# A two-block transformer kernel on one core: the output projection of the merged mixers split into two halves of its input rows

## What is computed

```
# one layer of the second block (hx, hc: normed and modulated latent and context tokens)
r_lat, r_ctx = bidirectional_scan(retention inputs)        # 4 heads of 128
g_lat, g_ctx = bidirectional_scan(gated linear attention inputs)   # 4 heads: keys 64, values 128
ret = from_heads(head_layernorm(r)) * silu(parts[3])       # 512 columns
gla = from_heads(rmsnorm(g, gla_norm_g)) * silu(parts[7])  # 512 columns
mx  = concatenate([ret, gla], axis=-1)                     # 1024 columns
x   = x + g1 * (mx @ w_out)                                # w_out: 1024 x 1024
x   = x + g2 * squared_relu_mlp(modulate(rmsnorm(x)), w_mlp1, w_mlp2)
```

## Time and profile before

| | us |
|---|---|
| runs | 3664.37, 3665.28, 3668.57 |
| profiled execution | 3674.53 |
| its span | 3672.7 |
| PE busy | 3476.8 (95%) |
| DVE busy | 2018.7 (55%) |
| ACT busy | 1198.1 (33%) |
| POOL busy | 213.0 (6%) |

### The profile page before, as it was taken

The page is one execution under the profiler, slowest core; times in us unless marked ns, Lnnn a source line. Parts: engine busy times, 40 slices in busy tenths (PEclk is TensorE's granted clock), DMA queues, the critical chain, the costliest instruction groups (busy, mean ns, idle before and its releaser), DMA issues.

```text
span 3672.7 us, 42155 instructions
## 1 busy us (share of the span) xinstructions
PE 3476.8 (95%) x17456; PEld 2763.4 (75%) x17456; DVE 2018.7 (55%) x3717; ACT 1198.1 (33%) x2005; POOL 213.0 (6%) x302
## 2 busy tenths in 40 slices
PE   7989999999989999998999879999998998889998
PEld 6647688887867688887986557888886885568886
DVE  5564588786654587784136754333235236654334
ACT  5353432225453432223112233322233112144332
POOL 0200000001130000000000001000001000000000
PEclk9999999999999999999999869999999998789999
DMA  5302244443202244443210011121222220113331
GB/s 168 105 19 86 69 151 159 152 135 98 65 29 89 69 150 159 151 136 131 83 56 31 22 53 56 58 69 58 62 65 87 100 70 18 41 51 99 93 102 59
DMA packets 214107, 317.00 MB, mean 86 GB/s; under 512 B 5304, under 2 KB 162618, under 8 KB 212636
## 3 DMA queue, kind: packets, MB, share of 16 engines
q1 hardware_dynamic: 198108, 243.00, 20.7%
q0 software_dynamic: 15808, 71.31, 5.8%
HBM read 300.66 MB, written 14.49 MB: 86 GB/s over the span
## 4 chain that ended last, share of the span: by engine, by line
PE 87%; DVE 7%; ACT 3%; issue 2%; DMA 1%; POOL 0%; SPq 0%; DVEq 0%; ACTq 0%; POOLq 0%
PE ps L94 86%; DVE t L115 3%; ACT t L100 3%; DVE t L107 2%; PE ps L97 1%; DVE t L111 1%; DVE t L121 0%; DVE t L112 0%; DVE ps L115 0%; DMA t<-gates_away 0%; DVE t L125 0%; DVE t L118 0%; DVE ps L107 0%; DMA t<-in_mem 0%; ACT L100 0%
## 5 line engine op out<-in xcount | busy, mean ns | idle before, releaser
L94 PE MATMUL ps<-t,t 128*128 128x512 f32 (+5 forms) x17040 | 3421.3, 366 | 165.2 <-DVE t L115 56.7
L94 PEld LDWEIGHTS ps<-t,t 128*128 128x128 f32 (+3 forms) x17040 | 2712.4, 190 | 848.0 <-issue 169.2
L100 ACT ACTIVATE t<-t 128x512 f32<-128x512 f32 (+4 forms) x1146 | 812.3, 744 | 1290.6 <-PE ps L94 932.5
L107 DVE TENSOR_TENSOR t<-t,t 128x1024 fp32r<-128x1024 f32 (+6 forms) x826 | 742.4, 927 | 591.9 <-ACT t L100 576.2
L100 ACT ACTIVATE t<-ps 128x512 f32<-128x512 f32 (+7 forms) x442 | 221.9, 529 | 809.6 <-PE ps L94 767.9
L115 DVE SCALAR_TENSOR_TENSOR t<-t,t,t 128x256 f32<-128x256 f32 (+3 forms) x927 | 437.6, 534 | 13.7 <-ACT t L100 7.3
L107 DVE TENSOR_TENSOR t<-ps,t 128x512 f32<-128x512 f32 (+4 forms) x293 | 188.6, 660 | 207.7 <-PE ps L94 142.6
L115 DVE SCALAR_TENSOR_TENSOR t<-ps,t,t 128x512 f32<-128x512 f32 (+1 forms) x228 | 139.8, 662 | 278.7 <-PE ps L94 258.5
L118 DVE COPY t<-ps 128x256 f32<-128x256 f32 (+3 forms) x162 | 73.1, 479 | 272.6 <-PE ps L94 252.9
L107 POOL TENSOR_TENSOR t<-t,t 128x64 f32<-128x64 f32 (+1 forms) x196 | 130.1, 689 | 1580.9 <-ACT t L100 1577.8
L100 ACT ACTIVATE t<-t,t 128x512 fp32r<-128x512 f32 (+3 forms) x160 | 96.1, 603 | 194.2 <-DVE t L107 127.8
(11 more groups left out here) (33 smaller groups left out, 294.7 us busy)
## 6 DMA issues: line engine op xcount, KB each, us to landing
t<-in_w_ff SPq DMA_DIRECT2D x64, 1024.0 KB, 5.4
t<-in_w_mlp SPq DMA_DIRECT2D x64, 1024.0 KB, 5.5
t<-in_ada_w POOLq DMA_DIRECT2D x48, 1024.0 KB, 5.9
t<-in_w_in SPq DMA_DIRECT2D x30, 1024.0 KB, 5.4
t<-in_w_qkv_o SPq DMA_DIRECT2D x12, 1024.0 KB, 5.2
t<-in_w_mem_kv SPq DMA_DIRECT2D x8, 1024.0 KB, 6.4
t<-in_w_mem_q SPq DMA_DIRECT2D x8, 1024.0 KB, 5.1
t<-in_w_mem_o SPq DMA_DIRECT2D x8, 1024.0 KB, 5.1
```

What stands on the lines that cost most here:

```text
L94: return Issued(self, self.e and self.e.matmul(o, l, r, start=start, stop=stop, skip_group_check=True))
L100: return Issued(self, self.e and self.e.activation(o, i, f, **kw))
L107: return Issued(self, self.e and self.e.tensor_tensor(o, a, b, op))
```

## The change

The projection is cut by its input rows. `U.out2r[l]` takes rows 0 to 511 (retention), `U.out2[l]` rows 512 to 1023 (GLA); each has two blocks of 4 input tiles by 512 columns, so two pairs a block. A pair of such a half has 4 kk x 2 tiles x 3 terms = 24 matmuls of 512 columns (and 24 of 256 in layer 0). The four pairs of retention's half are new units in the mixer's list: `product` (PE runs the pair, DVE and ACT do `start`) and `add` (DVE adds to the residual). GLA's half stays where the projection was. All of `add_to` is done twice, once for each half.

Retention's units gain a step `half` (the split into hi and lo, in place: the buffer `H.RH` lies over `H.Q` and `H.K`), and are spread over fewer units of GLA: all but the last 15 in layer 0 and the last 10 in layer 1. The squares of the sums use `SQ` in place of `H.KS`, so that `c_back` no longer waits for the last `gnormed`.

```diff
-    def feat(i, ms, segs, c0s=None):
+    def feat(i, ms, segs, c0s=None, bases=None):
...
-            base = 3 * setno[0]
+            base = 3 * setno[0] if bases is None else bases[x // 2]
...
-        U.out2[l] = [feat(i, two(b), segs) for b, i in enumerate(cols(A["w_out_2"][l], q4))]
+
+        U.out2r[l], U.out2[l] = ([feat(block(A["w_out_2"][l], k0, 4, 512 * b, 512), list(range(4 * b, 4 * b + 4)), segs,
+                                       None, bases) for b in range(2)]
+                                 for k0, bases in ((0, (0, 0) if l == 0 else (0, 2)), (4, None)))
...
-    H.KS = [place([128, S], F, YB + 2048 * i) for i in range(2)]
+
+    H.RH = place([128, 2, 4, T], R, D1)
...
-        n = len(g) - 8
+        n = len(g) - (15 if l == 0 else 10)
+        behind = ({("work", 1, 9): "o0", ("sum", 2): "a0", ("work", 1, 11): "o1", ("sum", 4): "a1 o2", ("sum", 6): "a2 o3",
+                   ("sum", 8): "a3"} if l == 0 else
+                  {("work", 1, 5): "o0", ("work", 1, 6): "o1", ("work", 1, 7): "a0 o2", ("sum", 1): "a1 o3", ("sum", 3): "a2",
+                   ("sum", 4): "a3"})
...
+        def out_half(u):
+
+            if u[0] == "product":
+                use = U.out2r[l][u[1] // 2]
+                feature(use, H.RH, lambda kk: [("clo", l, kk, z) for z in range(len(segs))], [use.pairs[u[1] % 2]])
+
...
+            elif u[0] == "half":
+                h, z = u[1:]
+                t0, n = segs[z]
+                act.wait_ge("fdone", l, h, z)
+                act.activation(H.RH[:, 0, h, t0:t0 + n], H.K[:, h, t0:t0 + n], ACT.Copy).then_inc("chi", l, h, z)
...
-            if u == ("work", 1, len(work) - 1):
-
-                act.wait_ge("gout", l, 1, *work[-1])
-                for k in range(4):
-                    for z, (t0, n) in enumerate(segs):
-                        act.wait_ge("fdone", l, k, z)
-                        act.activation(HR2[:, 0, k, t0:t0 + n], H.Q[:, k, t0:t0 + n], ACT.Copy).then_inc("chi", l, k, z)
...
+            elif u[0] == "half":
+                h, z = u[1:]
+                t0, n = segs[z]
+                dve.wait_ge("chi", l, h, z)
+                dve.tensor_tensor(H.RH[:, 1, h, t0:t0 + n], H.K[:, h, t0:t0 + n], H.RH[:, 0, h, t0:t0 + n].bitcast(F),
+                                  ALU.subtract).then_inc("clo", l, h, z)
+
...
+        def out_half(u):
+            use = U.out2r[l][u[1] // 2]
+            if u[0] == "product":
+                start(use)
+            else:
+                add_to(use, streams, lambda m, z: (("x_back", "c_back")[z], l), gain1, use.pairs[u[1] % 2])
...
             if l == 0:
                 pl.wait_ge("decay_log", l, 3, 3)
-                pl.wait_ge("gnormed", l, len(gla_sums(l)) - 1)
                 pl.wait_ge("fdone", l, 3, len(segs) - 1)
                 pl.dma_start(CX, A["c_away"].rearrange("p (k t) -> p k t", k=8)).then_inc(s_cback, "c_back", l)
```

More of the change, by code:

```diff
@@ L357, in program @@
         U.ff[l] = mlp(A["w_ff1"][l], A["w_ff2"][l], lat)
[L358 removed]
+    U.rq, U.rk, U.rv, U.rg, U.gq, U.gk, U.kt, U.gv, U.gg, U.gd, U.out2r, U.out2, U.ff2 = ({} for _ in range(13))
     for l in range(2):
@@ L493, in ret_units @@
         tasks, out_ = ret_tasks(l), []
-        steps = ([("mean", 0, 1), ("mean", 1, 2), ("var", 0, 3), ("end", 0, 5), ("var", 1, 5), ("end", 1, 6)] if l == 0 else
-                 [("mean", 0, 1), ("var", 0, 3), ("end", 0, 5)])
+        steps = ([("mean", 0, 1), ("mean", 1, 2), ("var", 0, 3), ("end", 0, 5), ("var", 1, 5), ("end", 1, 6), ("half", 0, 6),
+                  ("half", 1, 7)] if l == 0 else [("mean", 0, 1), ("var", 0, 3), ("end", 0, 5), ("half", 0, 5)])
         for h in range(4):
@@ L556, in mixed_units @@
             y = min(len(r), len(r) * (x + 1) // n)
+            out_ += [("out", ("product" if v[0] == "o" else "add", int(v[1]))) for v in behind.get(u, "").split()]
+        return out_
         return out_
@@ L575, in weights, with feature @@
             return [hl[:, a, :].rearrange("p (k n) -> p k n", k=u.kc) for a in range(2)]
-        def feature(u, x, ready_k):
+        def feature(u, x, ready_k, pairs=None):
             wv = weights(u)
-            for pair in u.pairs:
+            for pair in u.pairs if pairs is None else pairs:
                 for kk in range(u.kc):
@@ L1361, in project_out @@
                 start(u)
-                for m in two(b):
+                for m in [t.m for t in u.tiles]:
                     for s, (dst, n) in enumerate(streams):
@@ L1768, in hybrid_scalar @@
         for mixer, u in mixed_units(l):
-            (ret if mixer == "ret" else gla)(u)
+            {"ret": ret, "gla": gla, "out": out_half}[mixer](u)
         gla_high(len(sums) - 1)
         for z in range(2):
-            sq_free[z], rs_free[z] = ("rpv", l, len(tasks) - 1), ("fdone", l, 3, len(segs) - 1)
+            sq_free[z], rs_free[z] = ("gnormed", l, len(sums) - 1), ("fdone", l, 3, len(segs) - 1)
         streams = [(X, S), (CX, C)][:len(segs)]
@@ L1920, in attention, with add_to @@
                 prep(h, 4)
-        def add_to(u, streams, after=None, gain=None):
-            for t in u.tiles:
+        def add_to(u, streams, after=None, gain=None, tiles=None):
+            for t in u.tiles if tiles is None else tiles:
                 dve.wait_ge(*ready(u, t))
```

41 lines of the change are left out of this document (20 added, 21 removed).

## The result

The changed kernel takes 3695.45 us, the median of four runs (3687.69 to 3698.39). The kernel before took 3666.93 us beside it (3664.37 to 3673.72). The ratio is 1.0072, 95% interval 1.0051 to 1.0093: 0.7% slower, by some 26 us. The forecast was 3669 us with a range up to 3684. The measured time lies 11 us beyond that range. What was called within the noise (+3.8 us) is a clear loss of 26 to 29 us.

A forecast was written before the change was run, and what follows sets the result against it. The prediction took PE's matmuls, 87% of the chain, as the bound, so a change pays only where PE waits or runs slowly. Layer 0 +6.6 and layer 1 -2.8 gave +3.8 us on 3665.3: 3669 us, range 3648 to 3684.

The forecast's parts named there:

- The tail of layer 0: From work 8's end to the projection's end: 103.2 us plus 5 for the clock against 111.3, so -3.1 us.
- The four waits: Layer 0's tail: PE idle 3.0, 5.4, 4.6 and 5.8 us, 18.8 in all, each ended by DVE's adds.
- The clock term: Layer 0's tail: time lost at clock 0.50 after the four waits, 5 us within 0 to 9.3.
- The front of layer 0: Layer 0's mixer up to work 8: DVE takes on 11.4 us, partly in holes; +5 us within 0 to 11.4.
- theory O: From the experiments, not the forecast: layer 0's front lengthens by which unit an end stands in front of; order alone, 10 to 15 us.
- POOL's order in layer 0: The residual is issued before the last gates, so DVE waits for the gates: +4.7 us within 0 to 9.0.
- Layer 1: Tail +0.2, halves +3.5, gate wait gone -6.5: -2.8 us in all.
- The gain of 6.5 us that I booked for the wait: Layer 1's mixer: residual issued earlier, so PE's share of the wait for the gates goes; bounds 3 and 9 us.
- the 3.5 us that I had put against it: Layer 1's mixer: cost of the halves, where DVE waits for ACT's copy and subtracts; bounds 0 and 5.8 us.
- The base: Whole kernel: profiled execution 3674.5 us, median of the runs 9.2 us lower, so +3.8 us was added to 3665.3.
- Rival 2: Mixers of both layers: VectorE bounds, all 17.2 us of added work lands on the path, 3678 us; chance 0.20.
- Rival 3: Tails of both layers: the clock takes its full price, 9.3 + 6 us in place of 8, 3676 us; chance 0.10.

The follow-up runs named there:

- b1: The kernel before, unedited, run again for a profile nearer its median: 3666.93 us, -2.0 us (0.9997) against the kernel before beside it.
- a1: The changed kernel, unedited, run again: 3695.29 us, +25.7 us (1.0071) over the kernel before.
- b2: The kernel before with eight (layer 0) and four (layer 1) empty half units in retention's list, so only the order shifts: +7.2 us (1.0021) over the kernel before.
- a2: The kernel before with only retention's units spread over 15 (layer 0) and 10 (layer 1) fewer linear-attention units, not 8; no split: +12.4 us (1.0040) over the kernel before.
- d1: b2 with layer 0's retention ends and the steps behind them held past cumulations, states and work 0, in both directions: -0.7 us (0.9996) against the kernel before.
- d2: The changed kernel with all retention units held past work 0 from the first such end on, in layer 0's first direction: +19.7 us (1.0044) over the kernel before.
- d3: d2 with the same rule in layer 0's second direction too, the residual issued later: +21.5 us (1.0048) over the kernel before.
- c4: The changed kernel with POOL issuing the gates in front of the residual in both layers: +23.9 us (1.0061) over the kernel before.

## Why the prediction was wrong, step by step

**The tail of layer 0: right within 3.3 us, in part by luck.** Forecast -3.1 us. Measured -3.4 us between the two first traces (119.3 to 115.9) and +0.2 between b1 and a1. The four waits came where I had written them, each ended by DVE's adds: 1.9, 4.6, 3.9 and 5.1 us with the second short wait of each, 15.6 us for the forecast 18.8. The clock term was too small. I had taken it between what follows a wait of 2.04 us (3.4 us at 0.50) and one of 6.26 us (6.0 us), but each of these shorter waits was followed by 6.8 us at 0.50, with PE busy for 5.8 to 6.0 us of them. That is 2.9 to 3.0 us lost each time, 11.7 in all, not 5 within 0 to 9.3. In the first trace this came out even because the clock was at 1.00 from 2160.0 to the first of these waits: product 0 had no slow beginning, and PE was at that wait 18.1 us after work 8, not 21.5. In a1 the clock was low for longer there, and it took 20.9 us. Terms were off in opposite directions.

**The front of layer 0: wrong, and it decides the case.** Forecast +5 for DVE's added work, within 0 to 11.4, and +4.7 for the gates. Measured +23.6 (first traces) and +28.8 (b1 and a1). The step that failed is the one that took 5 us, within 0 to 11.4, for the 11.4 us of work that DVE takes on. It priced only the work that is moved in. It left out that the same edit moves every unit of retention past the units of linear attention. By the fronts of the traces:

- b2, the order shifted by the eight counted halves, no work added: +12.5 us. My bounds had no room for this at all.
- a2 over b2: +12.4 us, from 186.8 to 199.2. Up to the ends of head 0 both have the same order; from there a2's spacing is denser, two more ends (7.0 us of DVE) come into the front, and POOL's order is turned. The 12.4 us are 9.8 us of idle PE and 2.6 us of busy PE, and 5.9 us of the idle time stand behind the wait for the gates.
- the halves themselves: +3.9 us for 4.4 us of work. Here the method was right.

The sum is 28.8 us. It is a walk through four traces, not four independent prices: a2 has no counted halves, and the spacing alone takes its front 24.9 us over b1's. Half of b2's part returns when only the ends are moved off the states and work 0 (d1: 186.8 to 180.4). In the changed kernel, moving retention as a whole behind work 0 in one direction wins 10.6 us of front (d2, by its fastest run; 6 us by the medians). So theory O is shown for d1's part, and d2 bears it out. For the rest of what the denser spacing costs the cause stays open: part is the wait for the gates, and when d3 moved the other ends as well the time didn't follow. I had written that the weakest terms are the fronts, "where one order of two busy engines is replaced by another", and then gave them the bounds of an added piece of work.

**POOL's order in layer 0: right.** Forecast a wait of 4.7 us, measured 2.5 us on DVE in the first trace and 4.4 us in a1. Turning the order (c4) takes 3.3 us off the front.

**Layer 1: the mechanism came, the gain didn't.** Forecast -2.8 us; the first traces give -5.3 (front -3.9 for my -3.0, tail -1.4 for my +0.2). The wait for the gates is gone as forecast. But that the front agrees is luck: PE's idle time in it is 31.9 us before and after, and the 3.9 us are faster matmuls (125.4 to 121.5 us busy). The gain of 6.5 us that I booked for the wait was taken up by other waits, by more than the 3.5 us that I had put against it. And b1 is 6.8 us faster in this very mixer than the trace that I read. Against b1 the changed kernel is 2.5 us slower in layer 1. The PE wait that I took off existed in both traces of the kernel before (6.5 and 5.2 us). What differed was the clock around it.

**The base.** I took the 9.2 us between the profiled execution and the median as spread evenly, and subtracted them from the end. They weren't. The trace that I read is 6.4 us longer than b1's; it is 6.8 us longer in layer 1's mixer and 1.6 us in layer 0's, the stretches that the change edits, and shorter by 3.4 us ahead of them. In the pair a1 and b1 my terms come out as +28.8 for +9.7 (front of layer 0 with POOL's order), +0.2 for -3.1 and +2.5 for -2.8. So 19.1 of the missing 27.7 us are the front of layer 0, and 8.6 us are the tail and layer 1. The two traces are only 27.2 us apart, because a1 is 3.6 us faster ahead of layer 0's front and 0.7 us between the layers' stretches, in work that the change doesn't touch.

**The rivals.** Rival 2 (VectorE is the bound of the denser mixer) had the place and the sign, with 3678 us. Its price was the added work in full, 17.2 us. The engine was less of a bound than it says: DVE stands idle for 62 us of a1's front, more than in b1 (45). The two engines wait for each other in turn. Rival 3 took the clock's full price, but for the tails alone. In the Trainium skill, "TensorE: Matmul & The Clock Gate", section "HAM oscillation — how this bites in real kernels", bursts parted by waits are said to begin slowly each time. The rows at 2192.7 and 2209.7 agree: each burst after a wait began with 6.8 us at 0.50. In the front the slower matmuls are 35% (a1) and 69% (b2) of the loss over b1. I had counted the clock in the tails only.

## What to carry to other kernels

When two chains are interleaved by a rule that deals units out by number, an edit that adds units or changes the spacing reorders everything: price the new order stretch by stretch, and test it first with empty units. Keep long VectorE steps out of places where every next matmul needs VectorE too. What won time here was work put into a wait in pieces about as long as the wait, on banks of its own, and the transfer that is needed first issued first. Before a term of a forecast is called right, see in two traces whether the idle time or only the clock has moved.

## What was not expected of the hardware

The same program, with the same waits, can spend very different time at 1.2 GHz. The mixer of layer 1 of the kernel before took 157.3 us at a granted clock of 0.80 in one execution and 150.5 us at 0.83 in another, with 31.9 and 30.4 us of idle PE. Over b1's twelve runs the time goes from 3663.7 to 3678.8 us. A change of some microseconds should therefore be read from a trace that lies at the median, and from two traces of each kernel if possible.

The clock can pay or take more than the waits that an edit removes. Against a1, the front of d2 lost 2.5 us of waits and 8.1 us of busy time with the same matmuls. In d3, 9.5 us of waits went and 3.2 us of busy time came. Both are single traces, of d2's fastest run and d3's slowest. By the medians of their runs the two kernels are 1.8 us apart.
